# Two linear-attention branches: queries scaled in place of states, decay gates at another place in the vector queue, and the last right-hand sides in other buffers

## The reference, cut to what matters

```python
# GLA, one chunk (b = cumulative log decay in the chunk)
o = (q * exp(b)) @ S + attn @ v
S = exp(b_last) * S + (k * exp(b_last - b)).T @ v
# GDN, one chunk (gcum = cumulative log decay)
a   = -(k*beta) @ k.T * exp(gcum_i - gcum_j)          # strictly lower
rhs = concat([k*beta*exp(gcum), v*beta])
w, u = split(triangular_solve(I - a, rhs))
v_new = u - w @ S
o = (q * exp(gcum)) @ S + attn @ v_new
S = exp(g_last) * S + (k * exp(g_last - gcum)).T @ v_new
```

## Time and profile before

| | us |
|---|---|
| median of 3 runs | 2460.51 (2457.33 to 2462.3) |
| the profiled execution | 2454.73 |
| its span | 2452.5 |
| PE busy | 2286.6 (93%) |
| DVE busy | 1394.9 (57%) |
| POOL busy | 1119.6 (46%) |
| ACT busy | 576.7 (24%) |

### The profile page before, as it was taken

How to read it: one execution, slowest core, us unless ns; L and a number is a source line. 1 busy time by engine, 2 the same in 40 slices (tenths; PEclk the granted TensorE clock), 3 DMA queues, 4 the chain that set the end, 5 groups by cost and what they waited for, 6 DMA issues and landing times.

```text
span 2452.5 us, 34111 instructions
## 1 busy us (share of the span) xinstructions
PE 2286.6 (93%) x14110; PEld 1851.2 (75%) x14110; DVE 1394.9 (57%) x1999; ACT 576.7 (24%) x1167; POOL 1119.6 (46%) x642
## 2 busy tenths in 40 slices
PE   7999899999899999899999998998988878999998
PEld 5777687887776777687787756697887866788886
DVE  4445578567724444478767762486954664640532
ACT  2043321022232222222022040133534221210210
POOL 5521465765652222465766432163310056556664
PEclk9999999999999999899999999897988979999999
DMA  4210223424421110223433541021110002222321
GB/s 168 86 45 18 69 95 129 154 96 137 151 78 43 44 43 27 83 89 120 153 102 116 184 160 37 14 81 49 65 62 3 3 19 78 78 87 94 108 91 69
DMA packets 55001, 203.84 MB, mean 83 GB/s; under 512 B 6176, under 2 KB 6432, under 8 KB 53568
## 3 DMA queue, kind: packets, MB, share of 16 engines
q1 hardware_dynamic: 52272, 187.28, 23.1%
q0 software_dynamic: 1840, 11.70, 1.3%
q10 hardware_dynamic: 736, 2.69, 0.3%
HBM read 197.45 MB, written 4.19 MB: 82 GB/s over the span
## 4 chain that ended last, share of the span: by engine, by line
PE 87%; DVE 6%; ACT 2%; issue 2%; POOL 2%; DMA 0%; DVEq 0%; SPq 0%; POOLq 0%; ACTq 0%
PE bank L524 65%; PE bank L942 3%; PE bank L970 2%; PE bank L1550 1%; PE bank L1558 1%; PE bank L957 1%; PE bank L2332 1%; POOL parts_r L505 1%; PE bank L1528 1%; PE bank L2596 1%; PE bank L648 1%; PE bank L2328 1%; PE bank L946 1%; PE bank L2317 1%; PE bank L1377 1%
## 5 line engine op out<-in xcount | busy, mean ns | idle before, releaser
L524 PE MATMUL bank<-xn_r,parts_r 128*128 128x512 f32 (+1 forms) x2928 | 922.4, 393 | 33.1 <-DVE mix_r L725 14.3
L524 PE MATMUL bank<-big_r,parts_r 128*128 128x512 f32 x3208 | 935.8, 394 | 16.4 <-DVE big L886 8.9
L499 POOL TENSOR_SCALAR parts_r<-ring 128x1024 fp32r<-128x1024 f32 x293 | 333.3, 1138 | 1057.9 <-PE bank L524 1049.8
L505 POOL TENSOR_TENSOR parts_r<-ring,parts_r 128x1024 fp32r<-128x1024 f32 x293 | 735.9, 2512 | 24.4
L524 PEld LDWEIGHTS bank<-big_r,parts_r 128*128 128x128 f32 x3208 | 605.5, 190 | 149.6 <-DVE big L886 10.6
L524 PEld LDWEIGHTS bank<-xn_r,parts_r 128*128 128x128 f32 x2928 | 554.6, 191 | 153.8 <-issue 32.3
L849 ACT ACTIVATE big<-bank,small 128x512 f32<-128x512 f32 x88 | 68.3, 779 | 419.8 <-DVE big L893 251.3
L878 DVE TENSOR_TENSOR bank<-bank,nb 128x512 f32<-128x512 f32 x88 | 61.3, 699 | 148.8 <-PE bank L524 148.7
L2929 DVE TENSOR_TENSOR big<-big 128x512 f32<-128x512 f32 x32 | 82.6, 2585 | 71.0 <-ACT big_r L2910 71.0
L2855 DVE SCALAR_TENSOR_TENSOR h<-bank,vecs,h 128x512 f32<-128x512 f32 x24 | 17.9, 750 | 173.1 <-PE bank L524 173.1
L535 DVE TENSOR_TENSOR big_r<-big,big_r 128x512 fp32r<-128x512 f32 x76 | 105.6, 1391 | 0.4
(11 more groups left out here) (403 smaller groups left out, 2940.1 us busy)
## 6 DMA issues: line engine op xcount, KB each, us to landing
ring<-weights SPq DMA_DIRECT2D x295, 512.0 KB, 3.5
cst<-mod_w SPq DMA_DIRECT2D x48, 512.0 KB, 4.2
big<-consts POOLq DMA_DIRECT2D x3, 1024.0 KB, 7.6
cst<-consts SPq DMA_DIRECT2D x2, 1280.0 KB, 9.3
h<-x SPq DMA_DIRECT2D x8, 256.0 KB, 7.1
h_store<-h POOLq DMA_DIRECT2D x8, 256.0 KB, 2.3
big<-consts POOLq DMA_DIRECT2D x1, 2048.0 KB, 14.7
h<-h_store POOLq DMA_DIRECT2D x1, 2048.0 KB, 8.2
```

Source lines behind the costliest of these rows:

```text
L499: pool.tensor_scalar(rounded(unit_parts(u)[0]), ring[:, u % RING], 1.0, 0.0, ALU.mult, ALU.add)\
L505: pool.tensor_tensor(rounded(lo), ring[:, u % RING], value(hi), ALU.subtract).then_inc(part_ready, 1)
L524: mm = pe.matmul(ps, rounded(w[a]), rounded(x[b]), start=(start and n == 0), stop=(stop and n == 2))
```

## The change

The eight small products stand behind the first tile of gl_q and go to other banks; `glq_ps` gets a semaphore of its own. The nine DVE instructions for the GDN decays stand behind `gla_qk`. ACT makes scaled queries `gl_q2` with 32 copies of 128x64; PE's cross reads `gl_q2` and the state itself, of which there are now two buffers. Of the right-hand sides, number 9, 10 and 11 get buffers in the space of h, and numbers 6 to 11 are made behind the levels of the last group; the eight matmuls of `keep_busy` are gone. h comes back in step 1 of the recurrence.

```diff
 gates_pe:
+                    ps = grab(pe, GLZ_BANKS[i], *after("glz", i + 1))
...
-            fm_multi(pe, "gl_q", 2, [lat], "glq_ps", "glq")
...
+            fm_multi(pe, "gl_q", 2, [lat], "glq_ps", "glq", then=lambda f: decay_gates() if f == 0 else None)
 gates_dve:
-            dve.wait_ge(*after("gt_ln", 1))
-            link(dve, dve.scalar_tensor_tensor(out=z, in0=z, scalar=0.0, in1=az, op0=ALU.max, op1=ALU.add))
...
                 dve.tensor_tensor(gl_k2[:, dc], gl_k[:, dc % 2], gl_d[:, dc], ALU.mult).then_inc(sem("gla_qk"), 1)
+
+            dve.wait_ge(*after("gt_ln", 1))
+            link(dve, dve.scalar_tensor_tensor(out=z, in0=z, scalar=0.0, in1=az, op0=ALU.max, op1=ALU.add))
...
 gla_pe:
-                    pe.wait_ge(sem("gl_Sr"), 2 * (n - CCH) + d + 1)
+                    if d == 0:
+                        pe.wait_ge(*after("gl_S", n))
+                        pe.wait_ge(sem("gl_q2"), 1)
...
-                                       gl_Sr[(n - CCH) % 2][q:q + 64, dc, :], start=False,
+                                       gl_S[n % 2][q:q + 64, dc, :], start=False,
 gla_act:
             act.wait_ge(*after("gla_esc", 1))
+            act.wait_ge(*after("gla_qk", 4))
+            for dc in range(4):
+                for c in range(NCH - CCH):
+                    ins = act.activation(gl_q2[:, dc, c * CH:(c + 1) * CH], gl_q1[:, dc, c * CH:(c + 1) * CH], ACT.Copy,
+                                         scale=gl_sc[:, 0, dc * NCH + CCH + c:dc * NCH + CCH + c + 1])
+            ins.then_inc(sem("gl_q2"), 1)
 gla_dve:
+            dve.wait_ge(*after("gt", 1))
...
-                        dve.tensor_tensor(gl_Sr[m % 2][:, 2 * d:2 * d + 2], gl_S[:, 2 * d:2 * d + 2],
-                                          scol(0, d, steps(d)[n]), ALU.mult).then_inc(sem("gl_Sr"), 1)
...
+                if m >= 1:
+                    dve.wait_ge(*after("gl_x", 2 * m))
...
-                        ins = dve.scalar_tensor_tensor(out=gl_S[:, dc], in0=gl_S[:, dc],
+                        ins = dve.scalar_tensor_tensor(out=gl_S[(n + 1) % 2][:, dc], in0=gl_S[n % 2][:, dc],
 the inverse:
+        right = lambda i: gd_rs[i % 3] if i < 9 else gd_late[i - 9]
...
-                if q == GROUPS:
-                    keep_busy(pe, SETS, 8)
...
-                if i >= 3:
+                if 3 <= i < 9:
                     dve.wait_ge(dl("ups"), i - 2)
...
+            AHEAD = ((6,), (7,), (8,), (9, 10), (11,))
...
-                if q == GROUPS:
-                    decays_by_step()
...
+                    if q:
+                        for i in AHEAD[n - 1]:
+                            right_sides(i)
+                        if n == 1:
+                            decays_by_step()
 recur_pool:
-                        pool.wait_ge(dl("ups"), 2 * NBLK - 2 + d if n == 0 else 2 * NBLK)
+                        pool.wait_ge(dl("ups"), 7 + d if n == 0 else 2 * NBLK)
...
+                if n == 1:
+                    for k in range(KD):
+                        pool.wait_ge(sem(f"h_out{k}"), 16)
+                    pool.dma_start(h.rearrange("p k t -> p (k t)"), h_store[:, :]).then_inc(sem("h_back"), 16)
```

More of the change, by code:

```diff
@@ L477, in grab @@
             return bank[b]
[L479 to L484, removed]
         def take(pe, u):
@@ L783, in out_dve, with fm_multi @@
                 rstd_recip(dve, st + "n")
-        def fm_multi(pe, name, chunks, parts, full, read, blocks=KD):
+        def fm_multi(pe, name, chunks, parts, full, read, blocks=KD, then=None):
             u0 = UNITS[name]
@@ L797, in fm_multi @@
                 product_done[u0 + f] = after(full, (f + 1) * len(parts))
+                if then:
+                    then(f)
         ff_hi, ff_lo = part(0, KH, T), part(KH * T, KH, T)
@@ L1682, in gates_pe, with decay_gates @@
             fm_multi(pe, "ag", 1, [lat, ctxp], "ag_ps", "ag")
[L1683 to L1690, removed]
-            fm_multi(pe, "gl_q", 2, [lat], "glq_ps", "glq")
+            def decay_gates():
+                pe.wait_ge(*after("ag", 2))
+                for i in range(8):
+                    dc, p = divmod(i, 2)
+                    d, c = divmod(dc, 2)
+                    a, n = ((CTX, T), (0, CTX))[p]
+                    ps = grab(pe, GLZ_BANKS[i], *after("glz", i + 1))
+                    pe.matmul(ps[:, 0:n], gl_w2[32 * d:32 * d + GLA_RANK, c * P:(c + 1) * P],
+                              agT[32 * d:32 * d + GLA_RANK, a:a + n], start=True, stop=True).then_inc(sem("glz_ps"), 1)
+            fm_multi(pe, "gl_q", 2, [lat], "glq_ps", "glq", then=lambda f: decay_gates() if f == 0 else None)
             fm_multi(pe, "gl_k", 2, [lat, ctxp], "glk_ps", "glk")
@@ L1772, in gates_dve @@
                .then_inc(sem("gla_diff"), 1)
+            dve.wait_ge(*after("gla_diff", 1))
+            dve.wait_ge(*after("glq", 2))
+            dve.wait_ge(*after("glk", 4))
+            dve.wait_ge(*after("gla_ep", 1))
+            for dc in range(4):
+                c = dc % 2
+                dve.scalar_tensor_tensor(out=gl_q1[:, dc], in0=gl_q[:, c], scalar=GLA_DK ** -0.5, in1=gl_b[:, dc, CTX:TA],
+                                         op0=ALU.mult, op1=ALU.mult)
+            dve.wait_ge(*after("gla_en", 1))
+            for dc in range(4):
+                dve.tensor_tensor(gl_k2[:, dc], gl_k[:, dc % 2], gl_d[:, dc], ALU.mult).then_inc(sem("gla_qk"), 1)
             dve.wait_ge(*after("gt_ln", 1))
@@ L1787, in gates_dve @@
                                      op1=ALU.add).then_inc(sem("gt"), 1)
-            dve.wait_ge(*after("gla_diff", 1))
-            dve.wait_ge(*after("glq", 2))
-            dve.wait_ge(*after("glk", 4))
-            dve.wait_ge(*after("gla_ep", 1))
-            for dc in range(4):
-                c = dc % 2
-                dve.scalar_tensor_tensor(out=gl_q1[:, dc], in0=gl_q[:, c], scalar=GLA_DK ** -0.5, in1=gl_b[:, dc, CTX:TA],
-                                         op0=ALU.mult, op1=ALU.mult)
-            dve.wait_ge(*after("gla_en", 1))
-            for dc in range(4):
-                dve.tensor_tensor(gl_k2[:, dc], gl_k[:, dc % 2], gl_d[:, dc], ALU.mult).then_inc(sem("gla_qk"), 1)
         def steps(d):
@@ L2342, in right_w @@
                 for bb in range(2):
-                    r_ = gd_rs[(2 * u + bb) % 3]
+                    r_ = right(2 * u + bb)
                     for hd in range(GH):
```

53 lines of the change are left out of this document (21 added, 32 removed).

## The result

| | before | after |
|---|---|---|
| median of 4 runs each, us | 2461.41 (2457.33 to 2463.79) | 2429.21 (2428.18 to 2431.74) |
| ratio after to before | | 0.9876, 95% interval 0.9859 to 0.9893 |
| span of the profiled execution, us | 2452.5 | 2428.1 |

A forecast was written before the change was run, and what follows sets the result against it. PE, 87% of the chain of waits, was taken to bound the kernel, with DVE setting the beat in GLA's chunks. 8.0 + 3.3 + 15.1 + 1.6 = 28.0 us off the 2460.51 median gives 2432.5, range 2424 to 2444.

The forecast's parts named there:

- Gates: From the ag product to the keys' transposes: small products moved and clock staying high, less POOL waits, gain 8.0 us.
- The block: In the gates: the eight small products run together behind gl_q's first tile in 5.2 us, replacing a stretch of 10.9.
- Nothing from the moved gates: In the gates: moving the nine decay instructions later gives nothing by itself, since PE's own work covers it.
- Crosses: In GLA's chunks: a step takes 1.30 us instead of 1.77, over seven intervals a gain of 3.3 us.
- Inverse's end: Last level to recurrence: with all right-hand sides ready, the recurrence starts at 1952.5 instead of 1967.65, gain 15.1 us.
- Levels at no cost: In the inverse's levels: DVE's idle 2.7 us a level hides the right-hand sides made ahead; cost zero.
- Recurrence: At the recurrence's start: dense PE work in front keeps the clock high for a step and a bit, gain 1.6 us.
- its low end: In the recurrence: the lower limit of the predicted gain, none.
- the clock falls without the eight matmuls: Right-hand sides and recurrence: w and u run at the low clock, total gain only 20.6 us, 2439.9; chance 0.07.
- The rival of POOL and DVE in the gates: In the gates: POOL or DVE becomes the bound, costing 9.8 us, total gain 18.2, 2442.3; chance 0.07.
- that of exposed work: In the inverse's levels: the work put there is exposed, 7.6 us, total gain 20.4, 2440.1; chance 0.05.
- the best end of the range: For the whole kernel: fastest time allowed, 2424, from 1.1 and 2.9 us more gain and some 3 us of spread.

The follow-up runs named there:

- The fourfold work: Changed kernel with the two DVE multiplications of each of the six right-hand sides made ahead done four times: 2443.95 us, ratio 0.9935 to the kernel before.
- the recurrence filler: Changed kernel with useless matmuls in PE's gaps in the recurrence's first four steps: 2425.48 us; with more of them, up to step 5: 2427.23 us.
- two evictions: Changed kernel with ACT evicting gl_q's second tile between Exp and Ln, and one of the last unit's two u blocks: 2428.21 us, ratio 0.9892.

## Why the prediction was right

The mechanisms of the three large terms and their sizes came out; the nearness of the sum is partly luck, because errors in the gates cancel, the recurrence's term is not to be seen, and an untouched stretch gave time that I had not counted. Step by step:

- **Gates, 8.0 predicted, 8.1 measured.** The block took 4.24 us and not 5.2, so 6.7 us went with it and not 5.7. I had read the first four products as "partly at the low clock"; the granted clock was 1.00 from 1569.3 to 1572.1 us and fell behind them. The clock held behind the block, which gives back what I said (2.9 us; 6 us at 12 starts instead of 22 are rather 2.7). PE's waits for POOL, charged at 0.6, were 0.9, but 0.7 stood there before, so 0.2 more. Missed was the wait of 1.15 us for ACT: I had moved Exp and Ln earlier and not asked which eviction stands behind them on ACT. 6.7 + 2.7 - 0.2 - 1.15 = 8.1: the errors cancel. In the eight other profiles with the block the clock fell behind it for about 4 us, and none has that wait for ACT. Where the gates are untouched their stretch varies from 92.6 to 94.4 us (before is the longest), and with the whole change in them it is 86.3 to 87.3: 5 to 8 us.
- **Nothing from the moved gates**: 1.0003 alone. With the others they cost 1 to 2 us, against the 0.6 of the sum.
- **Crosses, 3.3 predicted, 4.1 measured.** The starts lie 1.77 us apart before (1682.53 to 1694.92, seven intervals), as read at one step, and 1.26 after instead of the assumed 1.30: 3.6 us. The other 0.5 is the last cross's own length, 0.58 us at the full clock against 1.18. The new copies on ACT, 32 of 0.333 us each, one every 0.24 us, took 7.7 us instead of at most 10.6, and no engine waited for them. The stretch in front of the first cross, 28.2 before and 28.9 after, is 24.7 to 29.3 over the profiles and tells nothing.
- **Inverse's end, 15.1 predicted, 15.2 measured**, alone and in the whole.
- **Levels at no cost**: 8.40 us each. The fourfold work shows that the slack is real, and where it ends.
- **Recurrence, 1.6 predicted, 0.0 measured** in this pair. This is the mis-sized term: its low end. I argued from what PE did ahead of it. The first phase did run at the full clock, but the second was at 1.2 GHz, as before. Over the profiles without the recurrence filler the stretch took 53.0 to 56.3 us in the six kernels that make the right-hand sides ahead (mean 54.0) and 54.1 to 56.4 in the five that don't (mean 55.2): about 1 us may be there, inside a scatter of 3. Filling the gaps brought 3.3 us, which is the gain that I had hoped for from dense work in front.
- **Not in the sum:** the untouched stretch from the last cross to the levels gave 5.1 us. PE's longest waits in it are the same in both (3.2 us for DVE ahead of the inverse, 1.8 for ACT's L2170); the clock is not, 0.91 in the mean before and 0.96 after. Two windows of before, behind its last cross, and one of after read

```profile
1696.00:1706.00 10.00, 10.00 (x41) 8.15 (x40) 7.93 (x17) 1.87 (x5) 2.93 (x2) 0.88 0.01 2
...
1736.00:1746.00 10.00, 10.00 (x52) 8.46 (x53) 8.57 (x16) 5.58 (x8) 1.18 (x1) 0.83 0.18 55
```
```profile
1690.00:1700.00 10.00, 10.00 (x45) 8.26 (x45) 9.14 (x18) 2.15 (x6) 4.05 (x2) 1.00 0.01 2
```

After has 1.00 in all of the first nine stretches of 10 us. Over all fourteen profiles the length of this stretch follows its mean granted clock: 118 us at 0.96 in six, 119.4 and 119.6 at 0.94, 121.0 to 121.9 at 0.92 to 0.93 in five, 123.2 at 0.91 in before. And it goes with one edit: eight of the nine profiles with the small products at their new place have 117.9 to 119.6 us, the ninth (two evictions) 121.3, and all five without it 121.0 to 123.2. So about 3 us of the launch's gain seem to come from there, through the clock of a stretch that no edit touches; why that clock is higher stays open. The other way, the untouched first part was 5.3 us longer in this profile. The 32 us of the medians against my 28 are within what these move.

Of the rivals, "the clock falls without the eight matmuls" describes the kernel before without them (33.0 us), and not the changed one, whose w and u stay at 1.50 and 1.47 us. The rival of POOL and DVE in the gates is answered by 0.9 us of waits for POOL and by decay instructions that end 6.7 us ahead of the masks; that of exposed work by levels of 8.40 us.

Two of my sums were loose: the best end of the range is 2432.5 - 1.1 - 2.9 - 3 = 2425.5 and not 2424, and 8.0 + 3.3 + 15.1 is 26.4 and not 27. The recurrence starts 26.0 us earlier (1941.64 against 1967.65).

## What to carry to other kernels

The useless matmuls that keep the clock up paid in their stretch as long as PE had gaps there, and cost their own time once real work filled the gaps: ask first whether the gap can go. Price the clock by what PE does inside a stretch too, and not only by what it did ahead of it. When a chain is moved earlier on an engine, list what is queued behind it there: here one eviction, 1.15 us in the one profile in which the clock held. Compare an untouched stretch over several profiles before its time is taken for a cost or a gain.

## What the hardware showed that I had not expected

- The granted clock fell to 0.50 1.6 us into the recurrence, behind 40 us of nearly full PE work at 1.00 and one wait of 1.98 us; PE then worked about 3 us of 5. In the five other kernels with the right-hand sides ahead and no filler there it fell 0.6 to 4.5 us into it. With about 1.8 us of filler a step it stayed at 1.00 through the first three steps in two of three profiles; in the third it fell in the first.
- Four microseconds of products with 16 rows, without a gap before or after, were followed by about 4 us at some 0.6 in eight of nine profiles; in the ninth the clock stayed at 1.00. Whether the few rows are the cause was not tested.
- The four DVE instructions of 128x512 that make the scaled queries took 8.5 us in all six profiles in which they stand behind the decay instructions, and 2.6 to 4.7 in the eight in which they stand ahead of them (3.45 in the changed kernel, 12 us earlier than before). POOL splits weights beside both; what makes the difference stays open.
- The untouched part up to the gates took 1559.4 to 1578.5 us over the profiles, with the same program: more than most single edits here are worth.
